# Folding the first load, the convolution set-up and the cache gathers of the sample tokens into neighbouring stages of a one-core decoder kernel

## The chip, the cores and the metric

The kernel is one program on one core of a Trainium2 chip. The metric is the time of one execution in microseconds (us). TensorE is called PE in the rows, VectorE DVE, ScalarE ACT, GpSimd POOL, and SyncE SP. SP computes nothing here; it issues the plain transfers. The gathers, which take their addresses from a table of indices, are issued by POOL.

## The reference, cut to what matters

The reference is one step of a two-layer decoder with 1024 prompt tokens and 32 sample tokens (8 sequences of 4). What the change touches is the first layer, whose mixer is a gated convolution beside a latent attention (MLA). The sample tokens attend over a paged cache of 8192 past positions, which is read through `page_table`:

```python
hp = rmsnorm(xp, norm_pre_mix[i]); hs = rmsnorm(xs, norm_pre_mix[i])
u = h @ w_in                                   # a_val, a_gate, a_g, c_q, kv, b_g
glu = a_val * jax.nn.sigmoid(a_gate)
ext = jnp.concatenate([conv_hist, glu], axis=1)
ya = jax.nn.silu(layernorm(causal_dwconv(ext, conv_w, conv_b), ln_w, ln_b))
...
past_ckv = cache_ckv[page_table, :, l].reshape(bs, past_len, KV_LORA)     # 8 x 8192 x 128
past_kr = cache_krope[page_table, :, l].reshape(bs, past_len, ROPE_DIM)   # 8 x 8192 x 32
s = (jnp.einsum('bqhc,bkc->bhqk', q_lat, ckv) + jnp.einsum('bqhr,bkr->bhqk', q_rope, krope)) * MLA_SCALE
p = jax.nn.softmax(where(k_pos <= q_pos, s, -inf)); o_lat = jnp.einsum('bhqk,bkc->bqhc', p, ckv)
```

## The kernel before

The program is a sequence of blocks. Inside a block each engine runs its own list of instructions and they wait for one another by semaphores; at a block's end all engines meet before any of them goes on. A transfer that was issued goes on across such an end, unless somebody in the block waits for its semaphore.

The first blocks are these. (a) A block that loads `ident`, then the activations `X` (nine tiles of 128 tokens by 1024, the ninth the 32 sample tokens) in three parts of 3, 3 and 2 tiles, and the sample tile. SP waits at its end only for `ident`. (b) `conv_setup`: SP loads the convolution state (`hs`), the taps (`wr`) and the bias (`cb`), and issues the first two weight blocks of 512 KB (`load`, line 723); PE transposes `hs` and `wr` (line 687 and 691), DVE copies the result away (700, 703). (c) `norm`: SP loads the gain (`gcol`, line 228), ACT sums squares tile by tile and waits for the part of `X` that holds the tile (`x_in`), POOL makes the reciprocal root (`rs`), DVE scales (`hn`, 286), PE transposes and DVE writes `HT` (268). DVE's first instruction of the block waits for `gcol`. (d) `even_front`, the input projection and the convolution, from 44.5 to 298 us.

Then comes `mla_prompt`. It computes queries, keys and values of the prompt and runs 64 units of attention (a unit is one head and 128 queries, in order of head pairs; 16 units make a pair): `scores` on PE counts the semaphore `m_sc`, then follow `maximum` (DVE), `exponent` (ACT), `normalise` (DVE), `turn` and `values` (PE). The queries of all heads stand in `Q`, which is the room `HT`.

`out_weights` issues the load of the 4096 KB output weights `WO` and of the gain `gb`, and waits for neither. `mla_sample` then loads the page table (`pt_i`) and constants, waits for all six (`d_c`), makes the index table `idx` on DVE, and gathers the cache on POOL in 32 pieces (4 for each sequence): a piece t is one gather of 1024 KB into `KC`, which lies in the room `HT`, and one of 256 KB into `RC`. Four pieces have room at a time, so piece t waits for the values of piece t-4 (`d_pv`). For each piece PE turns the rope part (`rope_turned`, line 1642) and the latent part (`turn`, 1653), makes scores (1660 and 1666), turns the probabilities (1677) and sums values (1686); DVE copies the turned keys (`key_out`, 1727). PE's list in iteration t is scores(t), turn(t+1), turned(t), rope_turned(t+2), values(t). Meanwhile SP loads `X` a second time (4224 KB), after it has waited for the constants; it is needed by the output projection, which comes after the sample tokens.

The rule that the kernel keeps for a piece's gather, in the issuing loop on POOL:

```python
for t in range(NCK):
    ch = t % NCH
    if t >= NCH:
        pool.wait_ge(d_pv, t - NCH + 1)
    ...
```

## Time and profile before

| | |
|---|---|
| runs shown | 3286.83, 3289.17, 3292.13 us (median 3289.17) |
| profiled execution: its time | 3295.15 us |
| profiled execution: its span | 3293.5 us |
| mean granted clock of PE | 0.903 of full speed |
| busy: PE, DVE, ACT, POOL | 2882.2, 1488.3, 765.9, 523.6 us |
| first piece of the sample attention on PE | 563.0 us |
| last copy of the sample attention on DVE | 747.8 us |

The span is from the first to the last instruction; the rest of the execution's own time, 1.65 us, lies around it. A row of the timeline is: start in us, duration in us, engine, line and operation, what is written and read, and in brackets how long the engine was idle before it and for whom. A row with x16 is 16 instructions merged. `SPq` is the issue of a transfer on SP; `HT` in a row can be the room that holds queries or cache pieces.

### The profile page before, as it was taken

To read this page: it belongs to the slowest core of one execution; us is meant where nothing else is said; L and a number is where in the kernel's file an instruction comes from. 1 tells how busy PE (TensorE), PEld (TensorE's weight loads), DVE (VectorE), ACT (ScalarE), POOL (GpSimd) and SP (SyncE) were. 2 spreads that over 40 slices of the span, in tenths; PEclk is the share of its full clock that TensorE was granted. 3 is DMA by queue.
4 is the path that set the end of the run, shared out by engine and by line. 5 is a ranking of instruction groups with operands and counts; after the bars stand their busy time and mean duration, and the time that the engine had idled before them with its cause. 6 is when DMAs were issued, how large, how long until landed. Compare 5 with 4: busy or idle time off the path is not lost. (4 is left out here: it accounts for less than half of the span.)

```text
span 3293.5 us, 40266 instructions
## 1 busy us (share of the span) xinstructions
PE 2882.2 (88%) x16179; PEld 2278.4 (69%) x16179; DVE 1488.3 (45%) x2523; ACT 765.9 (23%) x1435; POOL 523.6 (16%) x422
## 2 busy tenths in 40 slices
PE   5999895997978998988997798758999977899899
PEld 5997564776758976768997576435555535798576
DVE  4997664663411023345655310557777631102333
ACT  3222352332202221223221211111121210223121
POOL 1012001431202200122121001012212210220011
PEclk9999898997988997798998899778998978899879
DMA  3111004660041114103221221663334103211321
GB/s 106 51 33 44 14 1 174 234 216 4 1 132 53 48 68 153 51 1 87 85 88 61 82 95 46 196 192 96 83 89 113 16 13 115 70 46 71 128 83 47
DMA packets 235057, 270.60 MB, mean 82 GB/s; under 512 B 35926, under 2 KB 190102, under 8 KB 229667
## 3 DMA queue, kind: packets, MB, share of 16 engines
q1 hardware_dynamic: 215074, 179.82, 18.1%
q0 software_dynamic: 16384, 75.77, 6.5%
q10 hardware_dynamic: 3456, 12.98, 1.0%
q8 instruction: 105, 1.72, 0.2%
q14 instruction: 38, 0.31, 0.0%
HBM read 226.64 MB, written 41.28 MB: 81 GB/s over the span
## 5 line engine op out<-in xcount | busy, mean ns | idle before, releaser
L305 PE MATMUL pp<-HH,WS_part 128*128 128x352 f32 x1776 | 575.4, 324 | 0.0
L303 PE MATMUL pp<-HH,WH 128*128 128x352 f32 x1344 | 437.3, 325 | 40.0 <-POOL WS_part L442 40.0
L304 PE MATMUL pp<-HT_part,WH 128*128 128x352 f32 x1344 | 435.3, 324 | 0.0
L305 PEld LDWEIGHTS pp<-HH,WS_part 128*128 128x128 f32 x1776 | 337.4, 190 | 0.0
L303 PEld LDWEIGHTS pp<-HH,WH 128*128 128x128 f32 x1344 | 255.1, 190 | 42.0 <-POOL WS_part L442 42.0
L2717 PE MATMUL OP<-oWO,YT 128*128 128x512 f32 (+1 forms) x576 | 255.9, 603 | 3.3 <-DVE XE L2844 3.3
L304 PEld LDWEIGHTS pp<-HT_part,WH 128*128 128x128 f32 x1344 | 255.2, 190 | 0.0
L442 POOL TENSOR_TENSOR WS_part<-WS,WH 128x1024 fp32r<-128x1024 f32 x56 | 144.1, 2573 | 649.5 <-ACT WH L393 649.5
L2717 PEld LDWEIGHTS OP<-oWO,YT 128*128 128x128 f32 (+1 forms) x576 | 104.9, 184 | 146.4 <-issue 142.8
L2044 DVE TENSOR_REDUCE xmx<-xS 128x4 f32<-128x1024 f32 x16 | 19.5, 1219 | 377.0 <-PE xS L2005 377.0
L993 DVE SCALAR_TENSOR_TENSOR CV<-GXP,cw,CV 128x512 f32<-128x512 f32 x240 | 161.9, 742 | 0.0
L303 PE MATMUL pp<-HH,CK_part 128*128 128x352 f32 x432 | 142.0, 329 | 7.9 <-DVE HT_part L858 7.9
L304 PE MATMUL pp<-HT_part,CK_part 128*128 128x352 f32 x432 | 140.5, 325 | 0.0
L303 PE MATMUL zp<-WZH,HH 128*128 128x512 f32 (+1 forms) x288 | 114.6, 398 | 14.5 <-ACT ZS L2555 14.0
L303 PE MATMUL yp<-QT_part,KM_part 128*128 128x512 f32 (+1 forms) x288 | 115.9, 402 | 12.6 <-DVE WO_part L601 12.6
L304 PE MATMUL yp<-WO_part,KM_part 128*128 128x512 f32 (+1 forms) x288 | 115.6, 401 | 0.0
L305 PE MATMUL yp<-QT_part,SGX_part 128*128 128x512 f32 (+1 forms) x288 | 114.5, 398 | 0.0
L305 PE MATMUL zp<-WZH,HT_part 128*128 128x512 f32 (+1 forms) x288 | 113.9, 396 | 0.0
L304 PE MATMUL zp<-WZ_part,HH 128*128 128x512 f32 (+1 forms) x288 | 113.6, 394 | 0.0
L2698 POOL TENSOR_TENSOR XK<-XK,Db 128x2048 f32<-128x2048 f32 (+1 forms) x9 | 88.1, 9785 | 139.0 <-DVE XD L2870 139.0
L2397 DVE SCALAR_TENSOR_TENSOR oACC<-EP,cwo,oACC 128x1024 f32<-128x1024 f32 x72 | 98.6, 1370 | 9.2 <-DVE oACC L2395 2.4
L2763 PE MATMUL U<-XD,CBt 128*128 128x64 f32 (+1 forms) x576 | 83.4, 318 | 16.5 <-DVE CBt L2876 9.4
(495 smaller groups left out, 5383.3 us busy)
## 6 DMA issues: line engine op xcount, KB each, us to landing
WS<-x_w_qg SPq DMA_DIRECT2D x32, 512.0 KB, 3.9
HT<-cache_mem_k SPq DMA_DIRECT2D x16, 1024.0 KB, 5.1
HT<-cache_mem_v POOLq DMA_DIRECT2D x16, 1024.0 KB, 5.4
CBt<-cum_scratch SPq DMA_DIRECT2D x8, 2048.0 KB, 10.2
xbc_scratch<-oACC ACTq DMA_DIRECT2D x24, 528.0 KB, 2.7
WS<-o_w_in SPq DMA_DIRECT2D x24, 512.0 KB, 3.7
XT<-xbc_scratch SPq DMA_DIRECT2D x8, 1536.0 KB, 7.6
WS<-e_w_in SPq DMA_DIRECT2D x18, 512.0 KB, 4.0
```

Of the source, the lines that this page charges most:

```text
L303: nc.tensor.matmul(out, wh, xh, start=start, stop=False)
L304: nc.tensor.matmul(out, wh, xl, start=False, stop=False)
L305: return nc.tensor.matmul(out, wl, xh, start=False, stop=stop)
L442: nc.gpsimd.tensor_tensor(WL[:, k % slots, :, :], WS[:, k % slots, :, :], WH[k % 2][:, :, :], ALU.subtract).then_inc(p_lo, 1)
L993: ins = nc.vector.scalar_tensor_tensor(out=out, in0=src, scalar=tap, in1=out, op0=ALU.mult, op1=ALU.add)
L2044: dve_own.step(dve, nc.vector.tensor_reduce(mx[:, v, :], S[v][:].rearrange("p (h m) -> p h m", h=XH), AX.X, ALU.max))
L2397: ins = nc.vector.scalar_tensor_tensor(out=out, in0=src, scalar=tap, in1=out, op0=ALU.mult, op1=ALU.add)
L2698: nc.gpsimd.tensor_tensor(XK[R, :].rearrange("p (h e) -> p h e", h=SH), XK[R, :].rearrange("p (h e) -> p h e", h=SH), Db[R, :].unsqueeze(2 ...
L2717: m = nc.tensor.matmul(OP[hf][0:T, :], YT[:, k, 0:T], WO[:, k, hf * 512:(hf + 1) * 512], start=k == 0, stop=k == NX - 1)
L2763: m = nc.tensor.matmul(U[g % 2][R, e * SP_:(e + 1) * SP_], CB[R, h, R], XD[R, h * SP_:(h + 1) * SP_], start=True, stop=True)
```

## The change

The blocks (a) and (b) become one. SP's order in it is `ident`, the convolution's three loads, `X` in parts of 2, 3 and 3 tiles, the sample tile, the first two weight blocks. `norm` takes its tiles by the new parts. The page table and `c_piece` are loaded at the head of `mla_prompt`, DVE makes `idx` there behind the copies of the sample queries and ahead of `ln_gate`, and POOL gathers pieces 0, 1 and 2 during the attention, each when all scores of a head pair are done (piece t lies where the queries of that pair stood). Piece 3 is gathered at the head of `mla_sample`, the rest as before. PE no longer waits there for constants. The index tiles and `RC` get a fixed place at the end of SBUF. To make room, the squares of the layer norm (`lsq`) lie in the room of `V`, and those of the sample tokens in a small tile of their own, written by an ACT instruction of its own.

```diff
@@ -186,26 +186,15 @@
+    X_PARTS = (0, 2, 5, NQ)
 ...
-            part = slice(3 * k, min(3 * k + 3, NQ))
+            part = slice(X_PARTS[k], X_PARTS[k + 1])
 ...
-    with nc.Block() as block:
-        @block.sync
-        def _(sp):
-            sp.dma_start(ident[:], A["c_ident"]).then_inc(s_const, 16)
-            load_x(sp, x_in)
-            sp.wait_ge(s_const, 16)
-        @block.gpsimd
-        def _(pool):
-            pool_own.did(nc.gpsimd.memset(ones[:], 1.0))
-            pool_own.step(pool, nc.gpsimd.memset(mhalf[:], -0.5))
@@ -232,7 +221,8 @@
-                        act.wait_ge(x_in[i // 3], 32 if i // 3 == 2 else 16)
+                        k = (i >= X_PARTS[1]) + (i >= X_PARTS[2])
+                        act.wait_ge(x_in[k], 32 if k == 2 else 16)
@@ -636,6 +626,28 @@
+            RC, pt_i, piece, pt8, idx, ix, after = (
+                nc.alloc_sbuf_tensor_at(unique(n), shape, dt, offset=SAMPLE_AT + 4 * at) for n, shape, dt, at in (
+                    ("RC", [P, NCH, CT, ROPE], F32, 0), ("pt_i", [P, NB], I32, 2048), ("piece", [P, NCH], F32, 2056),
+                    ("pt8", [P, NB], F32, 2064), ("idx", [P, NB, NCH], U32, 2072), ("ix", [P, NCH], U32, 2104),
+                    ("after", [P, 1], F32, 2112)))
+            KCC = HT[:].rearrange("p k t -> p (k t)")[:, 0:NCH * CT * KV].rearrange("p (n k c) -> p n k c", n=NCH, k=CT)
+            ck = A["cache_ckv"].rearrange("n (s k) o c -> (n s) (k o c)", k=CT)
+            kr = A["cache_krope"].rearrange("n (s k) o c -> (n s) (k o c)", k=CT)
+            def gather(pool, t):
+                ch = t % NCH
+                nc.gpsimd.tensor_copy(ix[:, ch:ch + 1], idx[:, t // NCH, ch:ch + 1]).then_inc(d_ic, 1)
+                pool.wait_ge(d_ic, 2 * t + 1)
+                nc.gpsimd.tensor_tensor(after[:], ones[:, 0:1], ones[:, 0:1], ALU.add).then_inc(d_ic, 1)
+                for dst, src in ((KCC, ck), (RC, kr)):
+                    nc.gpsimd.indirect_dma_start(
+                        dst[:, ch, :, :].rearrange("p k c -> p (k c)"), None, src,
+                        bass.IndirectOffsetOnAxis(ap=ix[:, ch:ch + 1], axis=0)).then_inc(d_kc[ch], 16)
@@ -648,9 +660,9 @@
@@ -668,19 +680,24 @@
+                sp.dma_start(ident[:], A["c_ident"]).then_inc(s_const, 16)
 ...
+                load_x(sp, x_in)
 ...
+                pool_own.did(nc.gpsimd.memset(ones[:], 1.0))
+                pool_own.did(nc.gpsimd.memset(mhalf[:], -0.5))
 ...
+                pe.wait_ge(s_const, 16)
@@ -1120,11 +1137,12 @@
+    SAMPLE_AT = (nc.sbuf_usable_end - 4 * 2120) // 32 * 32
@@ -1132,7 +1150,8 @@
-            lsq, ldg = sb(c, "lsq", [P, 4, TOK]), sb(c, "ldg", [P, NQ + 1, P])
+            lsq, lsq_s = split_part(V, [P, 4, TP], dt=F32), sb(c, "lsq_s", [P, 4, SMP])
+            ldg = sb(c, "ldg", [P, NQ + 1, P])
@@ -1146,6 +1165,7 @@
@@ -1185,6 +1205,11 @@
+                pt_i, piece, _, _ = index
+                pages = A["page_table"].rearrange("b g -> g b")
+                for s in range(2):
+                    sp.dma_start(pt_i[s:P:2, :], pages).then_inc(d_i, 16)
+                sp.dma_start(piece[:], A["c_piece"]).then_inc(d_i, 16)
@@ -1241,10 +1266,10 @@
-                    pe.wait_ge(l_sq, 3)
+                    pe.wait_ge(l_sq, 4)
 ...
-                            m = nc.tensor.matmul(OB[SUM % 2][0:T, i:i + 1], lsq[:, ct, i * P:i * P + T], ones[:, 0:1],
+                            m = nc.tensor.matmul(OB[SUM % 2][0:T, i:i + 1], lsq[:, ct, i * P:(i + 1) * P] if i < NQ else lsq_s[:, ct, :], ones[:, 0:1],
@@ -1366,6 +1391,13 @@
+                pool.wait_ge(d_ix, 1)
+                for t in range(NCH - 1):
+                    pool.wait_ge(m_sc, 16 * (t + 1))
+                    if t == 0:
+                        pool.wait_ge(m_qr, 4)
+                    gather(pool, t)
@@ -1378,6 +1410,9 @@
+                        if b > TP:
+                            nc.scalar.activation(lsq_s[:], CV[:, :, TP:b], ACT.Square).then_inc(l_sq, 1)
+                            b = TP
@@ -1506,6 +1541,11 @@
+                pt_i, piece, pt8, idx = index
+                dve.wait_ge(d_i, 48)
+                dve_own.step(dve, nc.vector.tensor_scalar(pt8[:], pt_i[:], float(2 * NCH), None, ALU.mult))
+                nc.vector.tensor_tensor(idx[:], pt8[:].unsqueeze(2).to_broadcast([P, NB, NCH]),
+                                        piece[:].unsqueeze(1).to_broadcast([P, NB, NCH]), ALU.add).then_inc(d_ix, 1)
@@ -1562,7 +1602,7 @@
@@ -1577,63 +1617,38 @@
-                pt_i, piece = sb(c2, "pt_i", [P, NB], I32), sb(c2, "piece", [P, NCH])
-                pt8, idx, ix = sb(c2, "pt8", [P, NB]), sb(c2, "idx", [P, NB, NCH], U32), sb(c2, "ix", [P, NCH], U32)
-                KC = room[:].rearrange("p k t -> p (k t)")[:, 0:NCH * CT * KV].rearrange("p (n k c) -> p n k c", n=NCH, k=CT)
-                RC = sb(c2, "RC", [P, NCH, CT, ROPE])
 ...
-                after = sb(c2, "after", [P, 1])
 ...
-                    pages = A["page_table"].rearrange("b g -> g b")
-                    for s in range(2):
-                        sp.dma_start(pt_i[s:P:2, :], pages).then_inc(d_c, 16)
-                    sp.dma_start(piece[:], A["c_piece"]).then_inc(d_c, 16)
 ...
-                    sp.wait_ge(d_c, 96)
+                    sp.wait_ge(d_c, 48)
 ...
-                ck = A["cache_ckv"].rearrange("n (s k) o c -> (n s) (k o c)", k=CT)
-                kr = A["cache_krope"].rearrange("n (s k) o c -> (n s) (k o c)", k=CT)
 ...
-                    pool.wait_ge(d_ix, 1)
-                    for t in range(NCK):
-                        ch = t % NCH
+                    for t in range(NCH - 1, NCK):
 ...
-                        nc.gpsimd.tensor_copy(ix[:, ch:ch + 1], idx[:, t // NCH, ch:ch + 1]).then_inc(d_ic, 1)
-                        pool.wait_ge(d_ic, 2 * t + 1)
-                        nc.gpsimd.tensor_tensor(after[:], ones[:, 0:1], ones[:, 0:1], ALU.add).then_inc(d_ic, 1)
-                        for dst, src in ((KC, ck), (RC, kr)):
-                            nc.gpsimd.indirect_dma_start(
-                                dst[:, ch, :, :].rearrange("p k c -> p (k c)"), None, src,
-                                bass.IndirectOffsetOnAxis(ap=ix[:, ch:ch + 1], axis=0)).then_inc(d_kc[ch], 16)
+                        gather(pool, t)
 ...
-                    pe.wait_ge(d_c, 96)
@@ -1710,10 +1725,6 @@
-                    dve.wait_ge(d_c, 96)
-                    dve_own.step(dve, nc.vector.tensor_scalar(pt8[:], pt_i[:], float(2 * NCH), None, ALU.mult))
-                    nc.vector.tensor_tensor(idx[:], pt8[:].unsqueeze(2).to_broadcast([P, NB, NCH]),
-                                            piece[:].unsqueeze(1).to_broadcast([P, NB, NCH]), ALU.add).then_inc(d_ix, 1)
```

SP's list in the first blocks, before: `WS` are the weight blocks, `HH_part` the convolution's state and taps.

```order
L200 DMA ident<-c_ident 128x128
L194 DMA X<-x_prompt 128x3x1024 x2
L194 DMA X<-x_prompt 128x2x1024
L195 DMA X<-x_sample 32x1024
L197 UNCONDITIONAL_BRANCH
L669 UNCONDITIONAL_BRANCH
L671 DMA HH_part_78<-state_conv_a 120x2x512
L672 DMA HH_part_79<-e_conv_w 31x512
L673 DMA cb<-e_conv_b 128x4x1
L723 DMA WS<-e_w_in 128x8x128 x2
L665 UNCONDITIONAL_BRANCH
L226 UNCONDITIONAL_BRANCH
L228 DMA gcol<-norm_pre_mix 128x8x1
```

And after the change:

```order
L683 DMA ident<-c_ident 128x128
L684 DMA HH_part_58<-state_conv_a 120x2x512
L685 DMA HH_part_59<-e_conv_w 31x512
L686 DMA cb<-e_conv_b 128x4x1
L196 DMA X<-x_prompt 128x2x1024
L196 DMA X<-x_prompt 128x3x1024 x2
L197 DMA X<-x_sample 32x1024
L740 DMA WS<-e_w_in 128x8x128 x2
L677 UNCONDITIONAL_BRANCH
L215 UNCONDITIONAL_BRANCH
L217 DMA gcol<-norm_pre_mix 128x8x1
```

The three loads of the convolution stand ahead of `X` instead of behind it, and one block end (the branch L197 of before) is gone; the second, ahead of `gcol`, is still there.

POOL's list from the roots of the layer norm in `mla_prompt` to the first pieces of the sample attention, before:

```order
L1367 TENSOR_TENSOR lrs<-lms,mhalf 128x8
L1368 TENSOR_TENSOR lrs<-lms,mhalf 32x1
L1130 UNCONDITIONAL_BRANCH
L1614 UNCONDITIONAL_BRANCH
L1616 MEMSET QD 128x1024
L1624 COPY ix<-idx 128x1
L1627 TENSOR_TENSOR after<-ones 128x1
L1629 DMA HT<-cache_ckv,ix 128x2048
L1629 DMA RC<-cache_krope,ix 128x512
```

And after:

```order
L642 COPY ix_56<-idx_55 128x1
L645 TENSOR_TENSOR after_57<-ones 128x1
L647 DMA HT<-cache_ckv,ix_56 128x2048
L647 DMA RC_51<-cache_krope,ix_56 128x512
...
L647 DMA RC_51<-cache_krope,ix_56 128x512
L1148 UNCONDITIONAL_BRANCH
L1641 UNCONDITIONAL_BRANCH
L1643 MEMSET QD 128x1024
L642 COPY ix_56<-idx_55 128x1
```

Three pieces, each with its copy of the index, its small addition and its two gathers, stand ahead of the end of `mla_prompt` (the branch L1148) instead of behind the clearing of `QD`.

DVE's list at the head of the attention units, before:

```order
L1500 COPY X_part_3069<-PT_1 64x512 x2
L1502 COPY DTt_part_76<-S_1 128x8x8x4
L1506 COPY CUt_part_77<-HT 32x8x8x4 x4
L1464 TENSOR_TENSOR SG<-SG,CV 128x1056 x4
L1516 TENSOR_REDUCE nm<-S_1 128x1 x3
```

And after:

```order
L1537 COPY DTt_part_49<-S_1 128x8x8x4
L1541 COPY CUt_part_50<-HT 32x8x8x4 x4
L1546 TENSOR_SCALAR pt_1_54<-pt_i_52 128x8
L1547 TENSOR_TENSOR idx_55<-pt_1_54,piece_53 128x32
L1499 TENSOR_TENSOR SG<-SG,CV 128x1056 x4
L1556 TENSOR_REDUCE nm<-S_1 128x1 x3
```

The two instructions that make the index table stand ahead of the four products of `ln_gate`, and so ahead of the first maximum.

## Rows read from the trace of the kernel before

**Rows 1.** The page's first line.

```profile
span 3293.5 us, 40266 instructions
```

**Rows 2.** Timeline of the first 27 us.

```profile
5.16 12.04 SPq L723 DMA_DIRECT2D WS<-e_w_in  x2
...
19.92 1.86 PE L687 MATMUL ctp<-ident,HH_part 120*128 120x120 f32 x8 [19.92 <-DMA HH_part<-e_conv_w]
...
22.59 0.28 DVE L703 COPY cw<-ctp 128x124 f32<-128x124 f32 x1
...
23.14 0.37 SPq L228 DMA_DIRECT2D gcol<-norm_pre_mix  x1
...
25.70 0.15 DVE L276 TENSOR_SCALAR ms<-ss 128x1 f32<-128x1 f32 x1 [2.84 <-ACT HH_part L238]
...
26.87 0.15 DVE L276 TENSOR_SCALAR ms<-ss 128x1 f32<-128x1 f32 x1 [1.01 <-ACT HH_part L238]
```

**Rows 3.** Transfer rate from 14 to 24 us in 40 slices of 0.25 us.

```profile
GB/s 238 197 201 223 209 231 250 224 110 179 213 113 190 262 268 264 270 270 254 297 273 287 289 289 287 150 33 20 18 20 20 20 18 20 16 0 0 0 0 0
```

**Rows 4.** Timeline of `mla_prompt` and of the making of `idx`.

```profile
298.65 0.37 SPq L1188 DMA_DIRECT2D RG_part<-c_rope_cos  x1
...
323.63 0.53 DVE L1490 SCALAR_TENSOR_TENSOR RG_part<-S,RG_part 128x352 f32<-128x352 f32 x1 [0.88 <-PE S L1230]
...
376.37 4.76 DVE L1464 TENSOR_TENSOR SG<-SG,CV 128x1056 f32<-128x1056 f32 x4
...
382.40 0.47 PE L1328 MATMUL PT<-ident,RG 128*128 128x128 f32 x1 [5.04 <-DVE RG L1524]
...
550.78 0.17 DVE L1714 TENSOR_SCALAR pt<-pt_i 128x8 f32<-128x8 int32 x1 [15.98 <-DMA own<-c_own]
```

**Rows 5.** Timeline from the last attention units into the sample attention.

```profile
486.25 0.63 PE L1315 MATMUL S<-CAR,IDR 128*128 128x128 f32 x1
...
532.11 1.97 PE L1349 MATMUL OB<-RG,V 128*64 128x128 f32 x32 [0.88 <-DVE RG L1533]
...
536.47 4.68 SPq L1602 DMA_DIRECT2D pt_i<-page_table  x2
...
536.48 0.95 POOL L1616 MEMSET QD<- 128x1024 f32 x1 [196.90 <-POOLq L456]
...
551.10 1.23 DVE L1719 COPY QD<-CUt_part 32x256 f32<-32x256 f32 x4
...
562.96 1.09 PE L1642 MATMUL RTp<-ident,RC 128*128 128x128 f32 x4 [28.88 <-DMA RC<-cache_krope,ix]
...
567.50 0.69 DVE L1727 COPY QN<-KTp 128x512 f32<-128x512 f32 x1 [0.16 <-PE KTp L1653]
...
568.12 0.14 PEld L1642 LDWEIGHTS RTp<-ident,RC 128*128 128x128 f32 x1 [0.53 <-DMA RC<-cache_krope,ix]
...
568.95 1.06 PE L1666 MATMUL Sc<-QN,DTt_part 128*32 128x512 f32 x8
...
570.89 1.89 DVE L1727 COPY QN<-KTp 128x512 f32<-128x512 f32 x3
...
575.25 0.65 PE L1642 MATMUL RTp<-ident,RC 128*128 128x128 f32 x4 [2.05 <-DMA RC<-cache_krope,ix]
...
576.74 1.04 PE L1666 MATMUL Sc<-QN,DTt_part 128*32 128x512 f32 x8
...
577.62 0.99 POOL L1629 DMA_INDIRECT HT<-cache_ckv,ix  x1
...
580.81 0.60 PE L1642 MATMUL RTp<-ident,RC 128*128 128x128 f32 x4
...
582.24 1.04 PE L1666 MATMUL Sc<-QN,DTt_part 128*32 128x512 f32 x8
```

**Rows 6.** Windows: busy of PE, PEld, DVE, ACT, POOL, then PE clock.

```profile
537.00:540.00 3.00, 0.00 (x0) 0.00 (x0) 0.00 (x0) 0.00 (x0) 0.43 (x1) 0.52 1.00 404
...
566.00:569.00 3.00, 3.00 (x17) 2.15 (x19) 1.87 (x3) 0.00 (x0) 0.00 (x0) 0.69 1.05 422
```

More of the change, by code:

```diff
@@ L650, in even_mixer @@
                     even_front(c2, w_in, HT, HH, SG, QN, CV, GXP, GXS, cw, cb, WS, CK2, CKV, CKT, KRT)
-                mla_prompt(HT, QN, CKV, CKT, KRT, CV, SG, QLS, QRS)
+                mla_prompt(HT, QN, CKV, CKT, KRT, CV, SG, QLS, QRS, (pt_i, piece, pt8, idx), gather)
             out_w = out_weights(lay, A["e_w_out"][0], A["norm_post_mix"][0])
-            mla_sample(HT, QN, CKV, CKT, KRT, SG, QLS, QRS)
+            mla_sample(KCC, RC, gather, QN, CKV, CKT, KRT, SG, QLS, QRS)
             WOH = sb(lay, "WOH", [P, KT, D], F32R)
@@ L1121, in build, with mla_prompt @@
             "pv_done", "o_out", "q_sample_kept"))
-    x_again = layer_sem("x_loaded_again")
+    SAMPLE_AT = (nc.sbuf_usable_end - 4 * 2120) // 32 * 32
+    x_again, d_i = layer_sem("x_loaded_again"), layer_sem("pages_loaded")
     l_w, l_mm, l_cen, l_sq, l_ms, l_rs, l_dg, l_nrm, l_si = (layer_sem(n) for n in (
         "ln_loaded", "ln_filled", "ln_centred", "ln_squared", "ln_ms", "ln_rstd", "ln_diag", "ln_normed", "ln_silu"))
-    def mla_prompt(Q, QN, CKV, CKT, KRT, CV, SG, QLS, QRS):
+    def mla_prompt(Q, QN, CKV, CKT, KRT, CV, SG, QLS, QRS, index, gather):
         DH = NOPE + ROPE
@@ L1148, in mla_prompt @@
             OB = [pb(c, f"OB{a}") for a in range(2)]
+            assert nc.sbuf_base <= SAMPLE_AT
             block = c.enter_context(nc.Block())
@@ L1563, in build, with mla_sample @@
         "merge_mm", "merge_ev", "merge_exp", "merge_y", "merge_max_moved", "merge_max_back", "merge_w_loaded"))
-    def mla_sample(room, QN, CKV, CKT, KRT, SG, QLS, QRS):
+    def mla_sample(KC, RC, gather, QN, CKV, CKT, KRT, SG, QLS, QRS):
         NCK = NB * NCH
@@ L1595, in mla_sample @@
                 S = [pb(c2, f"Sc{a}") for a in range(2)]
+                assert nc.sbuf_base <= SAMPLE_AT
                 block = c2.enter_context(nc.Block())
```

## The prediction

> **What bounds the kernel now.** I read the page first: the span is 3293.5 us [rows 1], against 3295.15 us for the profiled execution, so 1.65 us lie around it, and I leave those as they are. PE is busy 88% of the span, so an edit is worth only what it takes out of PE's idle stretches or out of the chain that PE waits for. I then read the timeline where the change works.
>
> The first stretch is one chain of transfers. PE can't turn the convolution's state before 19.92 us, because it lies behind `X` in SP's queue; the set-up block ends with DVE's copy at 22.59 + 0.28 = 22.87 us; `gcol` is issued at 23.14; and DVE makes its first mean at 25.70 [rows 2]. The reader should also see SP itself: the issue of the two weight blocks takes 12.04 us, up to 17.20, since SP is held while the queue is full.
>
> The second stretch is the hole ahead of the sample attention. PE ends its last attention values at 532.11 + 1.97 = 534.08 and turns the first piece at 562.96, having been idle for 28.88 us for the gather [rows 5]. In it stand one behind the other: `WO`, the page table and the constants (DVE makes `idx` only at 550.78, after 15.98 us of waiting [rows 4]), then the gather.
>
> The third is the run-in: the first scores are at 568.95, the next at 576.74, the next at 582.24 [rows 5]. The last interval, 5.50 us, is the pace that the loop then keeps; the first is 7.79. PE waited 0.53 us (568.12) and 2.05 us (575.25) for gathers that share the engines with the second load of `X`, and its clock was low at first: 0.52 of full speed on average in 537 to 540, 0.69 in 566 to 569 [rows 6], so it stood at the lower of its levels (1.2 GHz) during the hole and came back to 2.4 GHz after about 3 us of work.
>
> **The first block.** The state now lands ahead of `X`, so the set-up's work on PE and DVE is over long before `X`. What then ends last is SP: the transfers ahead of the weights are the same in number and size, so SP should be held up to about 17.2 us as before. One block end less changes nothing in that. `gcol` is issued some 5.4 us earlier, at about 17.5 (22.87 to 23.14 gives 0.3 us for the end of a block). But it then stands behind the weights. The transfer rate drops from 287 to 33 GB/s at 20.6 us, yet a tail of 16 to 20 GB/s goes on up to 22.75 [rows 3], about a sixteenth of the 410 and more that `WO` and `X` reach (404 GB/s in [rows 6]), so I read it as one engine of sixteen that is late. `gcol` has a share on that engine too. Bounds: if it lands 2.56 us behind the tail, as from its issue at 23.14 to DVE's start at 25.70 [rows 2], DVE starts at 25.3 and the gain is 0.4; if no queue holds it, DVE starts at 17.5 + 2.56 = 20.1, gain 5.6. I take 1 us behind the tail, 23.7, since a queued transfer should pay only its own part of the 2.56: gain 2.0. ACT is then ahead with its squares, and DVE loses the wait of 1.01 us for the second mean [rows 2]; I take half, 0.5, because POOL's roots come in its place. Sum: **2.5 us**, bounds 0.4 and 6.6.
>
> **The page table in `mla_prompt`.** Three small transfers go ahead of the cosines. SP issues those at 298.65 and DVE wants them at 323.63 [rows 4]: 25 us of cover. When the page table was behind the 4 MB of `WO`, it and all constants were issued at 536.47 and there at 550.78, 14.3 us; it can't take more here. Cost 0; without the cover, up to 14. The extra ACT instruction for the sample squares is one small square, in a list that waits for PE between jobs: cost 0, bound 0.5. DVE's two instructions stand from 550.78 to the next copy at 551.10 in before [rows 4, 5], 0.32 us. Here they stand ahead of `ln_gate` (376.37), and PE and ACT wait for DVE there (PE 5.04 us until 382.40 [rows 4]), so they are paid: **-0.35 us**. Queued behind them are the gates and the first maxima.
>
> **The gathers during the attention.** Piece 2 is the last; it may go when the 48th scores are done, at 486.25 + 0.63 = 486.9 [rows 5], and is wanted at 536.5: 49.6 us of cover. A piece alone takes POOL four instructions of at most 1 us (0.99 for the larger gather, 577.62) and was wanted 8.7 us after that issue at the latest in steady state (577.62 to 586.3, which is 580.81 plus one pace). Cost 0, gain in the next part.
>
> One rule speaks against this. The Trainium skill (SBUF — State Buffer, "SBUF: two separate sides" and the part on a bandwidth-pool intuition behind it) says that DVE's two-port instructions shut GpSimd out of a shared port, so that gathers issued there starve for descriptors; it gives 620 ns alone against about 3100 beside a DVE copy. By it the issues would take some five times as long, an estimate of 5 us each for the larger gather, and the sum would not change within 49.6 us. No run here shows it so far; the one issue of [rows 5], at 577.62, took 0.99 us.
>
> **The head of the sample attention.** The block opens at 536.47 [rows 5]. PE can turn piece 0 at once. DVE waits for POOL's clearing (536.48 + 0.95 = 537.43), copies `QD` (1.23 us, to 538.7) and then four turned keys at 1.89/3 = 0.63 each, to 541.25. The scores of piece 0 start at about 541.4 instead of 568.95: **27.5 us**. In before, a key copy ended at 568.19 and the scores waited 0.76 us more for the transposes of the late piece, which are no longer there. The interval to the second scores falls from 7.79 to 5.50 us: **2.3 us**.
>
> From this comes off: (a) the clock. PE is idle only from 534.1 to 536.5, and in before it kept full speed to about 537.1 (a mean of 0.52 in 537 to 540 [rows 6]); but it works only in bits until 541. If the clock falls, about 3 us of work go at half speed; the bounds are 0 and 2.3, the whole excess of before. I take **-1.0**. (b) The transfers. Pieces 3 to 7 meet first `WO` and then `X`. Before, beside `X`, pieces 0, 1 and 2 were there at 562.96, 568.12 and 575.25 [rows 5], since PE waited for each: 5.2 and 7.1 us between them, 6.2 in the mean, against a pace of 5.50. Piece 3 is issued at about 538 and wanted at 541.4 + 5.5 + 4.1 = 551.0 (4.07 us from scores to `rope_turned`, 576.74 to 580.81): 13 us, enough even at twice 6.2. Pieces 5, 6 and 7 meet `X`, each 0.7 us slower than the pace: 2.1. Bounds: 0, if they keep to 5.2, and 5, if each takes 7.1: at half of the 422 GB/s of [rows 6] the 4.3 MB of `X` take 20.5 us, 3.3 pieces of 6.2, and 3.3 x 1.6 = 5.3. I take **-2.0**.
>
> For (b) the Trainium skill (DMA: Bandwidth & Descriptors, "Queues, rings and completion order") has a rule: an engine alternates between the queues that it has work for, packet by packet. With the 8 KB and 2 KB rows of a gather against the 4 KB rows of `X` this gives, as an estimate, 5.6 us for a piece and a loss of 0.3 instead of 2.0.
>
> **The sum.** 2.5 - 0.35 + 27.5 + 2.3 - 1.0 - 2.0 = 28.95, say 29 us. Against the profiled execution: 3295.15 - 29 = 3266.2. That execution was 6 us above the median of the runs shown, 3289.17, with the same work in it, so for the median I forecast 3289.2 - 29 = **3260 us**. Everything behind the sample tokens is only moved; the second `X` load ends earlier or at the same time and is wanted after 747.8 us.
>
> **The rivals.**
> - *Forecast*, gain 22 to 35 (lower: 0.4 - 1 + 29.8 - 2.3 - 5 = 22; upper: 6 - 0.35 + 29.8 = 35): 3254 to 3267. Chance 0.80.
> - *The gathers go late into the sample attention.* Piece 3 shares with 4 MB of `WO` and then `X` runs ahead of the rest. Speaks for it: the waits of 0.53 and 2.05 us. Against: 13 us of time for piece 3. It decides if piece 3 takes over 13 us. Price: 4 us for it, and 1.5 for each of four more, 10 instead of 2; gain 21 or less, 3268 to 3272. Chance 0.12.
> - *The head start isn't there.* The gathers go out only after the attention, since POOL is held by something, or PE waits in the new block for another thing. Then only the two loads of the page table are off the path: before, `WO` kept the queue up to about 548 anyway, so the gain is 3 to 5 us, 3285, within 0.2%. Against: the order of POOL's list and 49.6 us. Chance 0.03.
> - *Slower.* The gathers disturb the attention. Behind the 16th scores come 48 units, all with DVE, ACT and PE in one chain. To eat 29 us, each must take 0.6 us more; at 0.8 us it would be 38 and the kernel 9 us slower, 3298. Against: 3.9 MB are at most 3 x 6.2 us of transfer, in only a few units. Chance 0.02.
> - The rest, 0.03, is a gain of over 35, if the first block gives more than I can see.
>
> What a measurement of this kernel can tell from no change is about 0.2%, 6.6 us. Faster by more than that: 0.95; within: 0.03; slower: 0.02. The range 3252 to 3270 holds the forecast and part of the second case.
>
> **What would show it.** `gcol` issued near 17.5 and DVE's first mean near 23.7. DVE's two `idx` instructions ahead of `ln_gate`, and PE's wait there 0.35 longer. Three pairs of gathers during the attention, the last at about 487 us, each landed long before 536. PE's idle time ahead of its first turn of `RC` about 2.4 instead of 28.88 us, scores 0 some 5 us behind that turn, intervals of 5.5 us with at most two or three waits of a `rope_turned` for a gather, 2 us in all. The forecast is wrong if PE waits over 5 us for pieces 3 to 7, if `gcol` lands before 21, or if attention units get longer than they were.

## The result and the profile after

| | before | change |
|---|---|---|
| median (7 runs each) | 3289.17 us (3285.49 to 3293.24) | 3260.12 us (3250.29 to 3274.64) |
| ratio, 95% interval | | 0.991 [0.9887, 0.9933] |
| profiled execution, its span | 3295.15, 3293.5 us | 3266.82, 3265.2 us |
| mean granted clock | 0.903 | 0.908 |

The medians are 29.05 us apart; the interval of the ratio allows 22 to 37 us, and the forecast was 29. The profiled execution of the change is 28.3 us shorter. Its page begins:

```profile
span 3265.2 us, 40255 instructions
...
PE 2879.7 (88%) x16179; PEld 2277.3 (70%) x16179; DVE 1489.3 (46%) x2523; ACT 766.0 (23%) x1436; POOL 521.2 (16%) x422
```

The number of matmuls is that of before, so every matmul can be set against its counterpart by its number. I call **lead** the time by which an instruction starts earlier than in the profiled execution of before. The first stretch of the timeline, against [rows 2]:

```profile
5.77 10.35 SPq L740 DMA_DIRECT2D WS<-e_w_in  x2
...
8.39 1.83 PE L704 MATMUL ctp<-ident,HH_part 120*128 120x120 f32 x8 [8.39 <-DMA HH_part<-e_conv_w]
...
11.03 0.28 DVE L720 COPY cw<-ctp 128x124 f32<-128x124 f32 x1
...
16.57 4.02 SPq L217 DMA_DIRECT2D gcol<-norm_pre_mix  x1
...
24.48 0.21 DVE L266 TENSOR_SCALAR ms<-ss 128x1 f32<-128x1 f32 x2 [13.18 <-DMA gcol<-norm_pre_mix]
```

The set-up's work is over at 11.31 instead of 22.87. The block still ends only when SP is free of the two weight blocks, at 16.12. `gcol` follows at 16.57, and its issue itself takes 4.02 us; before it took 0.37, from 23.14. DVE starts 7.91 us behind that issue. It makes two means at one go (`x2`), so the wait between them is gone.

The timeline of `mla_prompt` with the index table, the first and the last of the early gathers, against [rows 4]:

```profile
372.44 0.42 DVE L1537 COPY DTt_part<-S 128x256 f32<-128x256 f32 x1 [1.20 <-PE S L1321]
...
374.16 0.17 DVE L1546 TENSOR_SCALAR pt<-pt_i 128x8 f32<-128x8 int32 x1
...
374.36 0.19 DVE L1547 TENSOR_TENSOR idx<-pt,piece 128x32 uint32<-128x32 f32 x1
374.47 4.76 DVE L1499 TENSOR_TENSOR SG<-SG,CV 128x1056 f32<-128x1056 f32 x4
...
413.74 1.22 POOL L647 DMA_INDIRECT HT<-cache_ckv,ix  x1 [0.42 <-issue]
415.26 0.96 POOL L647 DMA_INDIRECT RC<-cache_krope,ix  x1 [0.30 <-issue]
...
488.31 1.23 POOL L647 DMA_INDIRECT HT<-cache_ckv,ix  x1
489.85 0.95 POOL L647 DMA_INDIRECT RC<-cache_krope,ix  x1 [0.30 <-issue]
```

DVE did not wait for the page table. The timeline at the head of the sample attention, against [rows 5]:

```profile
532.88 1.97 PE L1374 MATMUL OB<-RG,V 128*64 128x128 f32 x32 [0.88 <-DVE RG L1573]
...
537.25 0.95 POOL L1643 MEMSET QD<- 128x1024 f32 x1 [46.45 <-POOLq L446]
...
537.29 1.05 PE L1657 MATMUL RTp<-ident,RC 128*128 128x128 f32 x4 [2.45 <-PEq L446]
...
538.13 0.41 SPq L1636 DMA_DIRECT2D own<-c_own  x1
...
542.56 1.06 PE L1681 MATMUL Sc<-QN,DTt_part 128*32 128x512 f32 x8
...
548.09 1.04 PE L1681 MATMUL Sc<-QN,DTt_part 128*32 128x512 f32 x8
...
557.80 1.43 SPq L196 DMA_DIRECT2D X<-x_prompt  x3
...
564.59 1.04 PE L1681 MATMUL Sc<-QN,DTt_part 128*32 128x512 f32 x8
...
572.00 1.11 PE L1657 MATMUL RTp<-ident,RC 128*128 128x128 f32 x4 [3.18 <-DMA RC<-cache_krope,ix]
...
574.75 1.11 PE L1681 MATMUL Sc<-QN,DTt_part 128*32 128x512 f32 x8
...
580.32 1.04 PE L1681 MATMUL Sc<-QN,DTt_part 128*32 128x512 f32 x8
```

PE's idle time of 28.88 us is 2.45, and its releaser is a block end (`PEq`) and no longer a transfer. Scores follow at 5.5 us, except once: between 564.59 and 574.75 lie 10.16 us. In that interval PE waits 3.18 us for piece 6, and it then works at half its clock for a while, as the windows show (busy of PE, PEld, DVE, ACT, POOL, then PE clock, share and rate of the transfers):

```profile
537.00:542.00 5.00, 4.71 (x22) 4.25 (x23) 3.49 (x8) 0.60 (x1) 3.21 (x5) 0.66 0.95 365
...
565.00:570.00 5.00, 3.82 (x30) 2.50 (x22) 3.47 (x7) 1.37 (x3) 2.18 (x4) 1.00 1.02 414
570.00:575.00 5.00, 3.00 (x40) 2.49 (x44) 0.00 (x0) 0.60 (x1) 0.00 (x0) 0.66 1.01 411
575.00:580.00 5.00, 5.00 (x56) 3.52 (x52) 3.63 (x7) 1.85 (x4) 2.31 (x4) 1.00 0.97 342
```

The same twelve transposes of a late chunk of the sample attention close that part, first in the trace of before, then in that of the change; the lead there is 737.21 - 713.29 = 23.92 us:

```profile
737.21 1.53 PE L1653 MATMUL KTp<-ident,HT 128*128 128x128 f32 x12
```

```profile
713.29 1.53 PE L1668 MATMUL KTp<-ident,HT 128*128 128x128 f32 x12
```

I call these twelve **the mark**. So of the 28.3 us of the two spans, 4.4 came behind the part that the change touches. What is known of them stands with the reasons, below.

### The profile page after: what moved, and what is told of

It reads as the page before. It is cut to its first block and busy times, and to the rows that moved or that the text cites. A ratio compares the mean times of both kernels' runs of the same rounds, so it can differ in the third digit from the quotient of the medians.

```text
span 3265.2 us, 40255 instructions
## 1 busy us (share of the span) xinstructions
PE 2879.7 (88%) x16179; PEld 2277.3 (70%) x16179; DVE 1489.3 (46%) x2523; ACT 766.0 (23%) x1436; POOL 521.2 (16%) x422
## 5 line engine op out<-in xcount | busy, mean ns | idle before, releaser
L293 PE MATMUL yp<-QT_part,KM_part 128*128 128x512 f32 (+1 forms) x288 | 115.2, 400 | 12.6 <-DVE WO_part L591 12.6
```

Source lines behind the costliest of these rows:

```text
L293: nc.tensor.matmul(out, wh, xh, start=start, stop=False)
```

## The experiments

**Theory A** is the prediction's: the hole went because pieces 0 to 2 are there early; the one wait at 572 is what `X` takes from the gathers beside it; and the first block gives little because `gcol` stands in SP's queue behind the weight blocks. **Rivals**: B, the three small loads of the page table, no longer behind `WO`, give the gain and the early gathers add little; C, the late piece 6 is the fault of `WO` and the constants and not of `X`; D, the gathers in the attention cost PE time there. All ratios are against the kernel before on the same chip, with 95% intervals. "Lead at the end" is the lead in the profiled execution at the mark; two further executions (below) show that it carries up to some 5 us of clock: the change stands there 23.92, 29.30 and 26.41 us ahead in its three executions, and before, executed again, 2.60 us behind.

### The two halves by themselves

The set-up part alone, on the kernel before:

```diff
+    X_PARTS = (0, 2, 5, NQ)
-    with nc.Block() as block:
...
+                sp.dma_start(ident[:], A["c_ident"]).then_inc(s_const, 16)
...
+                load_x(sp, x_in)
```

> The kernel before with the set-up part of the change alone (one block, the convolution's loads ahead of X, X in parts of 2, 3 and 3 tiles). Theory A (the set-up part is worth what the trace of the change shows at its end): DVE's first mean of the norm near 24.5 us instead of 25.70, the projection's first matmuls some 2 to 2.5 us earlier, and this lead is still there at the last matmul ahead of the attention; the whole is about 2.5 us faster than before, 0.999. Theory B (the attention's longer low stretch of PE's clock in the change comes from the gathers): here the attention keeps its length, and the low stretch at 374 us is 10.2 us as before. Theory C (it comes from where the attention begins against the clock): here the low stretch is 17 us too, though there are no gathers in the attention, and the attention is 2 to 3 us longer than before.

Measured: 3274.31 us, ratio 0.9944 [0.9918, 0.997]. DVE's first mean is at 23.99, and the lead at the end is 1.38 us. The hole stands as it was in its timeline:

```profile
23.99 0.21 DVE L267 TENSOR_SCALAR ms<-ss 128x1 f32<-128x1 f32 x2 [11.92 <-DMA gcol<-norm_pre_mix]
...
561.76 1.09 PE L1638 MATMUL RTp<-ident,RC 128*128 128x128 f32 x4 [28.80 <-DMA RC<-cache_krope,ix]
```

The measured gain, 18 us by the ratio, is far over the 1 to 2 us that the trace shows, so I ran the kernel once more:

> The kernel of e1 again, with five rounds. Its traced work is only 2.2 us shorter than before's once the low-clock time of busy PE is taken out, but its ratio in e1 was 0.9944. Theory A (the excess is the luck of PE's clock behind the sample attention): the ratio comes back to 0.998 to 1.000. Rival (starting the rest 2 us earlier changes systematically how long PE's clock stays low behind 730 us): the ratio is again below 0.997.

Measured: 3283.78 us, 0.9958 [0.9942, 0.9974]. That is 14 us by the ratio, smaller, but still more than the block explains. Theory A's 0.998 to 1.000 did not come; this is the rival's figure. The record of all executions says where the rest lies: the mean granted clock was 0.9092 and 0.9065 in the two sets of this kernel (6 and 11 executions), against 0.9034 and 0.9029 for before on the same chips (15 and 16). Within one kernel an execution whose clock is higher by 0.001 is some 2.5 us shorter (my fit over all of them, an estimate). At equal clock 4.5 and 3.3 us are left. At the mark the new trace stands 0.50 us behind that of before, where the first stood 1.38 ahead.

The gathers alone, with the first blocks of before:

```diff
-                mla_prompt(HT, QN, CKV, CKT, KRT, CV, SG, QLS, QRS)
+                mla_prompt(HT, QN, CKV, CKT, KRT, CV, SG, QLS, QRS, (pt_i, piece, pt8, idx), gather)
...
-                    for t in range(NCK):
+                    for t in range(NCH - 1, NCK):
```

> The change with the set-up of before: only the page table, the index table and the first three pieces are early. Theory A (the parts add up): PE's first turn of the sample attention comes 2.45 us behind its last work of the attention, scores of piece 0 some 5.3 us later, and at the end of the sample attention it stands 21 to 25 us ahead of before; the whole is 0.992 to 0.993. Theory B of e1 (gathers lengthen the attention): the attention is 2 to 3 us longer than before. Theory C: it has the length of before, 10.2 us low.

Measured: 3265.3 us, 0.9918 [0.9891, 0.9945]; lead at the end 26.24 us. PE waits 3.19 us for the same piece, at 569.45. So most of the change's gain is in this half (the expectation had the lead at 21 to 25), and the wait at 572 has nothing to do with the first blocks.

### The index table early, the gathers not

The loop goes from POOL's list in `mla_prompt` back to that in `mla_sample`:

```diff
-                for t in range(NCH - 1):
-                    pool.wait_ge(m_sc, 16 * (t + 1))
...
-                    gather(pool, t)
...
-                    for t in range(NCH - 1, NCK):
+                    for t in range(NCK):
```

> The change, but pieces 0 to 2 are gathered at the head of the sample attention too; the page table and the index table stay early. Theory A (the early gathers carry most of the hole): the first piece flows beside the 4 MB of WO and lands near 547 to 548 us, PE starts 10 us later than in the change and waits again for pieces 1 to 3, so that the end of the sample attention is 10 to 14 us later than in the change. Rival, as in the prediction (without early gathers only 3 to 5 us are left of the gain, because WO holds the queue up to 548): the end is 19 to 21 us later than in the change.

Measured: 3266.77 us, 0.9919 [0.9888, 0.9949]; lead at the end 11.68 us. PE's values end at 534.49, and the timeline goes on:

```profile
549.03 1.11 PE L1651 MATMUL RTp<-ident,RC 128*128 128x128 f32 x4 [14.54 <-DMA RC<-cache_krope,ix]
...
555.26 1.06 PE L1675 MATMUL Sc<-QN,DTt_part 128*32 128x512 f32 x8
...
560.31 0.66 PE L1651 MATMUL RTp<-ident,RC 128*128 128x128 f32 x4 [0.78 <-DMA RC<-cache_krope,ix]
```

From the end of PE's values to scores 0 are 34.87 us before, 20.77 here, 7.71 in the change. So the early index gives 14.1 us and the early gathers 13.1: rival B has half of the truth. The transfer of `WO` took 20.3 us from issue to landing here and 13.1 in before, so the first gather ran beside it. The medians of this run do not tell it from the change (3266.77 and 3260.12, whose runs reach from 3250.29 to 3274.64); the rows do.

### What makes piece 6 late

First `X` is held back until twelve pieces are done:

```diff
                     sp.wait_ge(d_c, 48)
+                    sp.wait_ge(d_pv, 12)
                     load_x(sp, [x_again] * 3)
```

> The change, with the second load of X issued as a whole once the values of piece 11 are done (near 604 us) instead of behind the constants. Theory A (the wait of 3.18 us ahead of the turn of piece 8 and the low clock after it come from X beside the gathers): no wait there, and one of 2 to 5 us appears between pieces 14 and 17, with the whole within 2 us of the change. Rival (WO, which is late on some engine, causes it): the wait stays near 572 us and none comes later.

Measured: 3255.19 us, 0.9875 [0.9838, 0.9913]. The wait at 572 is gone, though `WO` and the constants are where they were, and it is there again beside the moved `X` (timeline, then windows with the columns as above):

```profile
618.44 0.66 PE L1658 MATMUL RTp<-ident,RC 128*128 128x128 f32 x4 [2.86 <-DMA RC<-cache_krope,ix]
...
630.43 0.66 PE L1658 MATMUL RTp<-ident,RC 128*128 128x128 f32 x4 [0.77 <-DMA RC<-cache_krope,ix]
```

```profile
565.00:570.00 5.00, 5.00 (x66) 3.83 (x65) 3.14 (x8) 1.83 (x4) 1.84 (x4) 1.00 0.66 244
570.00:575.00 5.00, 5.00 (x65) 3.59 (x64) 3.14 (x7) 1.47 (x5) 1.84 (x4) 1.00 0.70 256
...
615.00:620.00 5.00, 2.14 (x46) 1.74 (x48) 0.84 (x2) 1.19 (x2) 0.00 (x0) 1.00 1.03 416
```

Without `X` the gathers move 244 to 256 GB/s and PE never idles; with it the transfers are full at 416 GB/s and PE has 2.14 us of work in 5. The lead falls by 4.07 us at that place (31.39 to 27.32), where the change lost 4.7. Theory A holds, rival C falls, and to move `X` as a whole gives nothing that can be told. (The expectation speaks of the turn of piece 8; the wait stands ahead of the turn of piece 6.)

Then `X` in nine pieces, one behind every second piece of the cache:

```diff
-                    load_x(sp, [x_again] * 3)
...
+                    for i in range(NQ):
+                        sp.wait_ge(d_pv, 2 * i + 8)
+                        sp.dma_start(X[:, i, :], tiles[:, i, :]).then_inc(x_again, 16)
...
```

> The change, with the second load of X in nine pieces of one tile, the first issued once the values of piece 7 are done and each next one two pieces later, instead of in one go. Theory A (a gather that is wanted 8.7 us after its issue bears 512 KB beside it, some 1.3 us, but not 4 MB): PE waits for no gather from piece 0 to 31, scores follow at 5.5 us throughout, and the sample attention ends 4 to 5 us earlier than in the change. Rival (any load beside the gathers costs its share of the transfer time): nine waits of about 0.5 us, no gain over the change.

Measured: 3259.38 us, 0.9898 [0.9875, 0.9921]. The loads are issued over 80 us, and PE's three waits are small (timeline):

```profile
583.69 79.77 SPq L1641 DMA_DIRECT2D X<-x_prompt  x8
...
604.83 0.66 PE L1661 MATMUL RTp<-ident,RC 128*128 128x128 f32 x4 [0.43 <-DMA RC<-cache_krope,ix]
...
616.31 0.66 PE L1661 MATMUL RTp<-ident,RC 128*128 128x128 f32 x4 [0.26 <-DMA RC<-cache_krope,ix]
...
639.19 0.66 PE L1661 MATMUL RTp<-ident,RC 128*128 128x128 f32 x4 [0.66 <-DMA RC<-cache_krope,ix]
```

The lead falls by 2.5 us there (31.85 to 29.35) instead of 4.7. So neither expectation came: there are waits, but three and not nine. Spreading saves some 2 us in this trace, of which 1.5 are the fall of the clock that the one long wait brought in the change; in the medians that can't be seen, and it did not come again together with the later weights (below).

### What holds the first block

First `gcol` goes ahead of `X`, into a place of its own:

```diff
+                sp.dma_start(g0t[:], A["norm_pre_mix"][0].rearrange("(k p) -> p k", p=P)).then_inc(n_g, 16)
                 load_x(sp, x_in)
...
```

> The change, with the norm's gain loaded ahead of X in the set-up block, so that DVE does not wait for it behind the weights. Theory A (the gain behind two weight blocks in SP's queue is what starts the norm): DVE's first mean at about 19.1 us, right behind ACT's first square, instead of 24.48; the projection starts some 5 us earlier than in the change. Rival (ACT or POOL set the start, the gain was not last): less than 1 us.

Measured: 3250.15 us, 0.9875 [0.985, 0.99]. DVE is no longer behind a transfer but behind ACT, which could start only behind the block end (timeline):

```profile
8.45 7.21 SPq L744 DMA_DIRECT2D WS<-e_w_in  x2
...
18.66 0.15 DVE L268 TENSOR_SCALAR ms<-ss 128x1 f32<-128x1 f32 x1 [7.38 <-ACT HH_part L230]
```

The first mean is 5.8 us earlier than in the change, the first matmul of the projection 5.4 (44.22 against 49.63), the lead at the end is 28.93. Then the issue of the weight blocks goes out of the set-up too, into `norm`'s block, where nobody waits for SP:

```diff
-                for n in range(2):
-                    load(sp, n)
...
+                    for n in range(2):
+                        weights(sp, n)
```

> As e6, and the two weight blocks are issued by SP in the norm's block instead of in the set-up block, so that SP is not held at the end of the set-up. Theory A (the set-up block ends last with SP, held by the full queue until 16.1 us): the norm's block opens at about 11.5 us, DVE's first mean at about 14, and the projection's first matmuls some 10 us earlier than in the change. Rival (the weights then land too late for the projection, or X itself is the bound): 5 us as in e6 and no more.

Measured: 3244.52 us, 0.9855 [0.9829, 0.9882], the lowest ratio on record. Its timeline:

```profile
11.44 5.01 SPq L746 DMA_DIRECT2D WS<-e_w_in  x2
...
14.00 0.15 DVE L271 TENSOR_SCALAR ms<-ss 128x1 f32<-128x1 f32 x1 [2.84 <-ACT HH_part L233]
...
20.91 1.06 ACT L233 ACTIVATE HH_part<-X 128x1024 f32<-128x1024 f32 x1 [1.67 <-DMA X<-x_sample]
```

The first mean is at 14.00, 10.5 us ahead of the change, and the first matmul of the projection at 39.62, 10.0 ahead. ACT now waits for `X` itself (0.47 and 1.67 us), but that doesn't set the pace: from the first mean to the first matmul of the projection the block takes 25.62 us here, 25.56 with the gain first and 25.15 in the change. So the whole gain is the earlier start. The lead at the end is 35.11 us.

### Both together

> e5 and e7 together. If both theories hold, 14 to 15 us are taken from the first 725 us of the change; with what PE's clock does behind it, the whole is 3240 to 3252 us, 0.985 to 0.989 of before.

Measured, with the edits of the spread `X` and of the later weights: 3243.48 us, 0.9865 [0.9838, 0.9891]; lead at the end 34.16. It is faster than before; its interval just touches that of the change, and it isn't told apart from the later weights alone. The whole time is as expected, but the 14 to 15 us over the change did not come: the lead at the end is 10.2 us larger than that of the change, and 8.8 with the clock taken out as below. The spread `X` adds nothing here. PE waits 1.27 us at 610.69 and 1.16 at 634.07, and the lead falls by 3.6 us over these pieces; with the later weights alone and `X` in one go it falls by 4.0.

### The same programs again

The profiled execution of the change had lost 2.67 us in the prompt attention, where the prediction put nothing, and I wanted to know whether the gathers (rival D) or the execution did it.

> The changed kernel, profiled once more. Theory A (PE's clock falls and comes back at its own times, so the same program differs by some us from one execution to the next, in the attention and behind the sample tokens): the head start at the end of the first projection and the restart 5.3 us behind the head of the sample attention are the same within 0.3 us, but the low stretch at 374 us can be 10 instead of 17 us, and the rest behind 725 us moves by up to 10 us. Rival (the 17 us stretch belongs to the change): it is there again, in this run and the next.

> The changed kernel, profiled a third time, with the same expectation as e9.

> The kernel before, profiled once more. Theory A of e9: the chain up to the norm, the hole of 28.9 us and its run-in are there again within 0.3 us, and its later stretches move by some us against the first profile as well. Rival: both profiles of before agree within 1 us at every place.

Measured: 3259.18, 3251.90 and 3300.71 us, beside 3288.33 for before on that chip. Windows of the attention's start, first before, then the change, then the change's second and third execution:

```profile
385.00:390.00 5.00, 5.00 (x28) 2.79 (x26) 3.23 (x9) 3.06 (x10) 0.00 (x0) 0.81 0.01 3
```

```profile
385.00:390.00 5.00, 5.00 (x15) 2.60 (x15) 1.86 (x5) 1.44 (x5) 0.00 (x0) 0.50 0.01 3
```

```profile
385.00:390.00 5.00, 4.86 (x39) 3.32 (x35) 2.94 (x9) 2.82 (x7) 0.00 (x0) 1.00 0.00 0
```

```profile
385.00:390.00 5.00, 5.00 (x31) 3.23 (x30) 2.87 (x8) 2.76 (x9) 0.00 (x0) 1.00 0.02 3
```

The clock fell to its lower level (1.2 GHz) in a stretch in which PE waited for DVE, and came back at different times: it stayed low for 17.1 us in the profiled execution of the change, 10.2 in before, 6.8 and 10.2 in the two further ones. The two further ones lose 0.35 and 0.31 us of lead from the copy of `DTt_part` to the last values, the index table's 0.32 included; the set-up part alone, without any early gather, lost 3.5. In the profiled execution of the change the whole loss falls between 386 and 390 us (lead 1.91 to -0.76), ahead of the first gather at 413.74; from there to the last values, with all three gathers between, the lead stays at -0.76. So rival D falls: the gathers cost the attention nothing that shows.

All this let me separate the clock from the rest. For each trace I added up the time in which PE was busy while its clock was at the lower level, and took half of it off, for the whole span and for the part up to the mark:

```
us                          span    busy at low clock   span - half   up to the mark - half
before                      3293.5  386.1               3100.4        718.2
before, again               3299.0  403.4               3097.3        718.2
change                      3265.2  381.7               3074.3        690.3
change, again               3257.5  365.7               3074.7        690.7
change, third               3250.2  355.2               3072.6        690.9
set-up part alone           3281.1  365.5               3098.3        716.1
set-up part alone, again    3293.9  391.5               3098.1        715.7
gathers alone               3263.9  375.8               3076.0        694.0
index early, no gathers     3266.5  357.1               3087.9        703.3
X late                      3259.5  368.3               3075.3        691.5
X spread                    3258.9  375.1               3071.4        689.9
gain first                  3250.3  367.0               3066.8        685.5
weights later               3251.2  375.1               3063.6        680.8
both together               3242.5  352.3               3066.4        681.8
```

Three executions of one program lie 15 us apart in the span, 2.1 in the third column and 0.6 in the last; the two of before 5.5, 3.1 and 0.0. By the third column the change is worth 25.0 us, the set-up part alone 0.7 and the gathers alone 22.9; by the last, the sharper one, 27.6, 2.3 and 24.2. Beyond the set-up part, the early index gives 12.6 of it and the early gathers 12.7. To move `X` costs 0.9 there, to spread it gives 0.7 alone and -1.0 with the later weights: nothing that can be told. The correction is an estimate, since it takes PE as the bound wherever PE is busy. At the head of the sample attention of before that isn't so: PE works from 562.96 to 567.86 at the lower level and then waits for the next piece (568.12, [rows 5]). So up to 2.4 us have to be added to the change's 27.6.

## Why the prediction was right, step by step

The terms, in the order of the sum, against the profiled executions:

| term | predicted | measured | from |
|---|---|---|---|
| first block | +2.5 | +1.63, and +0.85 of clock | first projection matmul 51.26 to 49.63; lead 2.48 at matmul 400 (1.86 and 2.17 in the further executions) |
| index table on DVE | -0.35 | -0.32 | lead 2.22 at the copy of `DTt_part`, 1.90 at `ln_gate` |
| prompt attention | 0 | -2.67 | lead 1.90 to -0.77 at the last values, lost while the clock was low |
| hole, with the clock | 27.5 - 1.0 | +27.16 | 34.87 to 7.71 |
| first interval | +2.3 | +2.26 | 7.79 to 5.53 |
| transfers | -2.0 | -4.73 | intervals 10.16 and 5.57 against 5.50 |
| to the end of the sample attention | +28.95 | +23.92 | with -0.26 of small steps between 104 and 374 us |
| behind it | 0 | +4.4 | to the end of the span |

**The mechanism** is shown: the early gathers and the early index take out the hole, half each. **The sum** was right about the part that it speaks of, and right to 0.1 us by luck. At the mark the profiled execution had 5.0 us less than the forecast; the leads of all three executions of the change and the two of before differ by 27.8 us in the mean, 1.1 less than the forecast. Corrected for the clock the part up to the mark is shorter by 27.6 to 30.0 us, against 28.95 + 1.0 = 29.95 of the terms without the clock's. Behind the mark, where nothing was changed, the three executions took 2539.4 to 2551.9 us and those of before 2556.3 and 2559.2. That remainder, which the forecast put at 0, scatters by more than 10 us, so it is chance that the medians are 29.05 apart.

**Terms mis-sized.** (1) The transfers. The prediction spread -2.0 over pieces 5 to 7; they took 4.73 at one place. 3.18 us of it is PE's wait for piece 6, and the rest the clock, which fell in that wait. From issue to landing the larger gather of piece 5 took 5.75 us, those of pieces 6 and 7, beside `X`, 10.0 and 9.75, so they were 4 us late and not 0.7. The bound of 5 held; the value, and the sign "2 us in all", were too small and had no clock in them. The prediction also has the second `X` load end "earlier or at the same time". SP issued it at 557.80 (550.77 in before), since the constants, issued by 538.13, landed 19.7 us later behind 4 MB of `WO` and the gather; its last part landed at 579.9 instead of 575.6, still long before it was wanted. (2) The first block. `gcol` did pay only "its own part of the 2.56": it landed 0.4 us behind the second weight block. But that block, issued from 6.45 on, landed at 24.07 (23.26 in before), and the prediction had the tail end at 22.75. So DVE's mean came at 24.48 instead of 23.7, and the gain there is 1.2 and not 2.0. The further executions have 23.95 and 24.07. The wait of 1.01 us was gone. (3) The clock at the head. PE's clock is 0.66 in 537 to 542, and the stretch costs 0.35 us instead of 1.0, since PE has little to do in it. The prediction read the return of the clock in before as "about 3 us of work"; the 0.69 of 566 to 569 [rows 6] puts it at 567.86, 4.9 us after PE's restart. (4) The rival "only the two loads are off the path" was put at a gain of 3 to 5 us, because `WO` "kept the queue up to about 548 anyway"; the early index by itself gives 14.1 us there and 11.7 at the end. The gather ran beside `WO` and did not come after it: piece 0 was there at 549.03, and `WO` landed at 555.8. (5) The attention was put at 0 with no range for the clock. The zero is right for the gathers; the execution added -2.67.

**Two rules, weighed.** The three early gathers were issued in 1.22, 1.22 and 1.23 us each, and landed 5.90, 5.77 and 5.79 us behind the start of the issue; later ones, with no bulk load beside them, took 0.99 us to issue and landed after 5.5 to 5.8. The Trainium skill (SBUF — State Buffer, "SBUF: two separate sides", and the part on a bandwidth-pool intuition behind it) has a transfer issued by GpSimd that starves for descriptors beside DVE's copies, some five times as long; no gather of this trace shows that. Nor is the quarter by which the issue was longer shown to be DVE's doing: the first gather of before took 1.22 as well (551.93), and the one at 538.75 in the change took 0.99 beside DVE's copies from 538.24 to 542.22. The wait for piece 6 was 3.18, 2.88 and 3.00 us in the three executions of the change, 3.19 with the gathers alone, 2.74 with the gain first and 2.61 with the later weights. By the alternation between queues of the Trainium skill (DMA: Bandwidth & Descriptors, "Queues, rings and completion order"), with 8 KB and 2 KB rows against 4 KB, the loss was estimated at 0.3 us; the traces speak against that estimate and for the row of 7.1 us between pieces of [rows 5]. The estimate took one row for one packet, while that section has a packet hold some 9 to 17 descriptors, so it is the estimate that falls, and the rule is not tested.

**What stays open.** Every changed kernel had a higher mean granted clock than before, and part of that lies in regions that it doesn't change. Behind the mark PE was busy at the lower clock for 348 and 360 us in the two traces of before and for 315 to 336 in those of the change, for 326 and 348 in those of the set-up part alone, and for 310 to 342 in the others. The two traces of the set-up part alone don't agree, but over all executions its mean granted clock was higher in both sets, so this isn't one lucky execution. Why an earlier start should shift the phases in which the clock falls, these runs don't show.

## What to carry to other kernels

Put a small load for which a block waits ahead of the bulk loads of its queue, and issue bulk loads in a block where nobody waits for the issuing engine: here these two moves were worth 10 us on the first block, against 1.6 to 2.2 for the merged block itself. When a stage begins with a chain of table, index and gather, issue the whole chain in the stage ahead as soon as its room is free, and look at the index by itself, which gave half of the gain here. A bulk load beside the gathers costs its wait wherever it stands; neither to move it nor to spread it gave anything that can be told from nothing. Judge such edits by the lead of one instruction right behind the place, over several executions, and take half of PE's busy time at the lower clock off, since the whole time varies by more than many an edit.

## What the runs showed of the hardware that was not expected

- The issue of a small transfer isn't always short: `gcol` took SP 4.02 us in the change, right behind the weight blocks, and 0.51 ahead of `X`, where the three parts of `X` behind it took 4.67 instead of 1.63. The same two weight blocks held SP for 12.04 us in before and for 10.35, 7.21 or 5.01 in the others, least where they were issued last.
- The clock fell in PE's wait of 3.18 us (0.66 in 570 to 575), and this cost some 1.5 us more than the wait itself. With the held-back `X` PE had waited 2.86 us at 618.44, and the window of 615 to 620 shows 1.00; with the later weights it had waited 2.61 at 561.68, and 560 to 565 shows 1.00. It is the same kind of wait, with and without a fall.
- One program, executed three times, had PE busy at the lower clock for 355 to 382 us, and its spans differ by 15 us; with half of that busy time taken off they agree within 2.1.
